# Softmax denominators of an eight-head attention: last four probability tiles summed by one strided reduction, in four pieces

## The reference, cut to what matters

```
s = einsum(qn, k_nope) + einsum(qr, k_rope)      # 1024 keys x 1024 queries for each head
p = softmax(s * scale, axis=-1)                  # exp(s - max) / sum over the keys of exp(s - max)
o = einsum(p, v)                                 # (1024 queries, 64) for each head
```

## Time and profile before

| | |
|---|---|
| median of 3 runs | 1615.19 us (1614.73 to 1616.01) |
| profiled execution, its own time | 1616.77 us |
| its span, first to last instruction | 1614.9 us |
| PE busy | 1500.5 us, 93% |
| DVE busy | 1072.1 us, 66% |
| ACT busy | 713.2 us, 44% |
| POOL busy | 426.7 us, 26% |
| mean granted TensorE clock | 0.968 |

### The profile page before, as it was taken

The page is one execution under the profiler, slowest core; times in us unless marked ns, Lnnn a source line. Parts: engine busy times, 40 slices in busy tenths (PEclk is TensorE's granted clock), DMA queues, the critical chain, the costliest instruction groups (busy, mean ns, idle before and its releaser), DMA issues.

```text
span 1614.9 us, 15669 instructions
## 1 busy us (share of the span) xinstructions
PE 1500.5 (93%) x5798; PEld 996.8 (62%) x5798; DVE 1072.1 (66%) x1022; ACT 713.2 (44%) x688; POOL 426.7 (26%) x209
## 2 busy tenths in 40 slices
PE   6999999999999999887899991799999999999997
PEld 3444587844344444444448871588888888887774
DVE  4533235433724656788766558598999998998886
ACT  3310000035503214433342442477777777777773
POOL 0031000000011006476764424022332222332204
PEclk9999999999999999999899995799999999999999
DMA  9311120206000000000013229699999999999994
GB/s 322 116 53 52 59 97 1 56 15 135 23 0 1 0 0 26 1 26 1 26 65 119 91 93 372 228 349 378 378 379 374 373 378 378 378 379 379 367 381 198
DMA packets 152886, 284.45 MB, mean 176 GB/s; under 512 B 25301, under 2 KB 35875, under 8 KB 152836
## 3 DMA queue, kind: packets, MB, share of 16 engines
q1 hardware_dynamic: 147219, 263.32, 45.9%
q0 software_dynamic: 4464, 16.25, 3.8%
q10 hardware_dynamic: 1152, 4.19, 0.6%
HBM read 259.10 MB, written 24.64 MB: 176 GB/s over the span
## 4 chain that ended last, share of the span: by engine, by line
PE 76%; DVE 11%; DMA 5%; issue 3%; ACT 2%; POOL 1%; SPq 0%; POOLq 0%; DVEq 0%; ACTq 0%
PE psum L1146 14%; PE psum L1602 9%; PE psum L1604 9%; PE psum L1603 9%; DMA arena<-in_exp_w_down 4%; PE psum L1377 4%; PE psum L1239 3%; PE psum L1127 3%; PE psum L1347 2%; PE psum L1092 2%; PE psum L1513 2%; PE psum L1439 2%; DVE arena L1917 2%; PE psum L1515 2%; PE psum L1514 2%
## 5 line engine op out<-in xcount | busy, mean ns | idle before, releaser
L2110 DVE TENSOR_TENSOR split_at<-arena,split_at 128x2048 fp32r<-128x2048 f32 x188 | 427.6, 2290 | 62.5 <-ACT split_at L1008 61.4
L1008 ACT ACTIVATE split_at<-arena 128x2048 fp32r<-128x2048 f32 x192 | 367.7, 1916 | 69.5 <-PE psum L1604 52.5
L1602 PE MATMUL psum<-split_at,split_at 128*128 128x512 f32 x768 | 305.9, 398 | 1.4 <-DVE split_at L2116 1.4
L1604 PE MATMUL psum<-split_at,split_at 128*128 128x512 f32 x768 | 300.2, 391 | 0.0
L1603 PE MATMUL psum<-split_at,split_at 128*128 128x512 f32 x768 | 299.5, 390 | 0.0
L1146 PE MATMUL psum<-arena 128*128 128x512 f32 x512 | 224.7, 594 | 1.4 <-DVE arena L1859 1.4
L1146 PEld LDWEIGHTS psum<-arena 128*128 128x128 f32 x512 | 96.1, 190 | 124.0 <-issue 123.9
L1604 PEld LDWEIGHTS psum<-split_at,split_at 128*128 128x128 f32 x768 | 144.5, 188 | 31.3
L1602 PEld LDWEIGHTS psum<-split_at,split_at 128*128 128x128 f32 x768 | 144.7, 188 | 29.7 <-DVE split_at L2116 1.8
L1603 PEld LDWEIGHTS psum<-split_at,split_at 128*128 128x128 f32 x768 | 144.9, 189 | 28.4
L639 POOL COPY arena<-arena 128x1 uint32 (+1 forms) x14 | 28.3, 2021 | 361.2 <-DVE arena L2144 361.2
(11 more groups left out here) (303 smaller groups left out, 2299.3 us busy)
## 6 DMA issues: line engine op xcount, KB each, us to landing
arena<-in_exp_w_gate SPq DMA_DIRECT2D x64, 1024.0 KB, 14.8
arena<-in_exp_w_up SPq DMA_DIRECT2D x64, 1024.0 KB, 14.2
arena<-in_exp_w_down SPq DMA_DIRECT2D x64, 1024.0 KB, 14.3
arena<-in_w_in SPq DMA_DIRECT2D x9, 1024.0 KB, 8.5
arena<-in_x SPq DMA_DIRECT2D x8, 512.0 KB, 6.6
xhat_scratch<-arena SPq DMA_DIRECT2D x8, 512.0 KB, 9.9
arena<-in_w_out SPq DMA_DIRECT2D x8, 512.0 KB, 3.6
arena<-xhat_scratch SPq DMA_DIRECT2D x8, 512.0 KB, 4.7
```

The source lines that it names most:

```text
L1008: a(flat(wsplit[c % WS][0]), wraw[:, c], ACT.Copy).then_inc(s_whi, 1)
L1602: mm(bank(out_bank), src[0][:, k, :], whi[:, k % 4, :], start=(k == 0), stop=False)
L1604: ins = mm(bank(out_bank), src[1][:, k, :], whi[:, k % 4, :], start=False, stop=(k == KT - 1))
L2110: tt(flat(lo), wraw[:, c], flat(hi), ALU.subtract).then_inc(s_wlo, 1)
```

## The change

Five things are changed together.

1. DVE's three additions of tiles 4 to 7 are replaced by four `tensor_reduce` instructions. Each reads all four `p_at` tiles for 256 queries with the tile index innermost (consecutive elements lie 4096 bytes apart in a partition), adds the four, and writes 256 columns of `p_last`. All four wait for the head's last exponential and stand behind `max_rows(h + 1)`.
2. ACT's exponentials of units 0 to 3 of a head now wait for all four pieces of the head before (`s_da` at `4 h`).
3. `sums_inverse` writes its result back into bank 7; `o_scale` reads it there and not from SBUF. The PE waits that protect bank 7 are on `s_ov` (the scaling) and no longer on `s_oi` (the inverse). `o_scale(h - 1, 0)` stands ahead of `max_rows`, `o_scale(h - 1, 1)` behind the pieces.
4. `p_first` has two buffers, by head parity. POOL's first addition waits for the sums of head `h - 2`.
5. `sum_probs(h, 0)` moves from the end of head `h` into head `h + 1`, directly ahead of `sum_probs(h, 1)`. SP's loads into `gin`, `bin_` and `xres` wait for head 6's sums.

```
-        p_first, p_last = mem(27600, T), mem(29648, T)
-        o_raw, o_inv = mem(30672, 2, HALF), mem(52176, 2, HALF)
+        p_first, p_last = [mem(28624, T), mem(27600, T)], mem(29648, T)
+        o_raw = mem(30672, 2, HALF)
...
-            sp.wait_ge(s_exp, TT * (NH - 1))
+            sp.wait_ge(s_sum, 2 * NH - 2)
...
-                if i == 0 and h:
-                    pool.wait_ge(s_sum, 2 * h - 1)
+                if i == 0 and h >= 2:
+                    pool.wait_ge(s_sum, 2 * h - 2)
...
-                        act.wait_ge(s_da, 3 * h - 3 + max(kb, 1))
+                        act.wait_ge(s_da, 4 * h)
...
                 if part == 0:
                     pe.wait_ge(s_pa, 3 * h + 3)
                     if h:
-                        pe.wait_ge(s_oi, 2 * h)
+                        pe.wait_ge(s_ov, 2 * h)
                 else:
-                    pe.wait_ge(s_da, 3 * h + 3)
+                    pe.wait_ge(s_da, 4 * h + 4)
...
                         if m == 0 and h:
+                            sum_probs(h - 1, 0)
                             sum_probs(h - 1, 1)
...
-                sum_probs(h, 0)
                 if more:
                     scores(TT * h + TT)
                     scores(TT * h + TT + 1)
+            sum_probs(NH - 1, 0)
             sum_probs(NH - 1, 1)
...
                 if i == 0:
-                    pe.wait_ge(s_oi, 2 * NH)
+                    pe.wait_ge(s_ov, N_OUT + 4)
...
-                v.reciprocal(o_inv[:, h % 2, cols], bank(7)[:, cols]).then_inc(s_oi, 1)
+                v.reciprocal(bank(7)[:, cols], bank(7)[:, cols]).then_inc(s_oi, 1)
...
-                   o_inv[half, h % 2, c0:c1], ALU.mult).then_inc(s_ov, 1)
+                   bank(7, 1, DV * j, DV * j + DV)[:, c0:c1], ALU.mult).then_inc(s_ov, 1)
...
+            def add_probs(h, c):
+
+                v.wait_ge(s_exp, TT * h + TT)
+                if h:
+                    v.wait_ge(s_sum, 2 * h)
+                cols = slice(256 * c, 256 * c + 256)
+                v.tensor_reduce(p_last[:, cols], p_at[:, :, cols].rearrange("p b t -> p t b"), AX.X, ALU.add).then_inc(s_da, 1)
...
-                add_probs(h, 0)
-                if h + 1 < NH:
+                if h:
+                    o_scale(h - 1, 0, 0, HALF)
+                if more:
                     max_rows(h + 1)
-                add_probs(h, 1)
-                add_probs(h, 2)
+                for c in range(4):
+                    add_probs(h, c)
                 if h:
-                    for j in range(2):
-                        o_scale(h - 1, j, 0, HALF)
+                    o_scale(h - 1, 1, 0, HALF)
```

More of the change, by code:

```diff
@@ L577, in add_probs @@
                 pool.wait_ge(s_exp, TT * h + i + 2)
-                if i == 0 and h:
-                    pool.wait_ge(s_sum, 2 * h - 1)
+                if i == 0 and h >= 2:
+                    pool.wait_ge(s_sum, 2 * h - 2)
                 if i:
                     pool.wait_ge(s_pa, 3 * h + i)
-                first = p_at[:, 0, :] if i == 0 else p_first
-                pool.tensor_tensor(p_first, first, p_at[:, i + 1, :], ALU.add).then_inc(s_pa, 1)
+                total = p_first[h % 2]
+                pool.tensor_tensor(total, p_at[:, 0, :] if i == 0 else total, p_at[:, i + 1, :], ALU.add).then_inc(s_pa, 1)
             for h in range(NH):
@@ L1447, in sum_probs @@
                     if h:
-                        pe.wait_ge(s_oi, 2 * h)
+                        pe.wait_ge(s_ov, 2 * h)
                 else:
-                    pe.wait_ge(s_da, 3 * h + 3)
+                    pe.wait_ge(s_da, 4 * h + 4)
                 for j in range(2):
-                    ins = mm(bank(7, 1, DV * j, DV * j + DV), ones[:, 0:DV], (p_first, p_last)[part][:, HALF * j:HALF * j + HALF],
+                    ins = mm(bank(7, 1, DV * j, DV * j + DV), ones[:, 0:DV], (p_first[h % 2], p_last)[part][:, HALF * j:HALF * j + HALF],
                              start=(part == 0), stop=(part == 1))
@@ L1966, in o_scale @@
                 tt(yT_at[DV * (h % 2):DV * (h % 2) + DV, h // 2, HALF * j + c0:HALF * j + c1], o_raw[half, h % 2, c0:c1],
-                   o_inv[half, h % 2, c0:c1], ALU.mult).then_inc(s_ov, 1)
[L1969 to L1975, removed]
+                   bank(7, 1, DV * j, DV * j + DV)[:, c0:c1], ALU.mult).then_inc(s_ov, 1)
[5 more added lines that the diff above has]
+                v.tensor_reduce(p_last[:, cols], p_at[:, :, cols].rearrange("p b t -> p t b"), AX.X, ALU.add).then_inc(s_da, 1)
             for h in range(NH):
-                slots = (ROUGH_AT if h else ROUGH_AT_0) if h + 1 < NH else {}
+                more = h + 1 < NH
+                slots = (ROUGH_AT if h else ROUGH_AT_0) if more else {}
                 if h == 0:
```

## The result

The changed kernel takes **1634.2 us** (median of 4 runs, 1632.62 to 1635.97) against 1615.41 for the kernel before in the same session. The ratio is 1.0117, with a 95% interval from 1.0099 to 1.0134: 18.8 us slower. The forecast was 1604.6, faster. The measured time lies in the rival that the prediction called *something between* (1623 to 1637, chance 0.12).

The account below looks back on a forecast made before the run. DVE alone was taken to set the stretch at head boundaries, where PE stands waiting. From the median 1615.2 us: -26.0 + 3.3 + 4.4 + 7.7 = -10.6, so 1604.6; own range 1597 to 1611, full range 1597 to 1654.

Parts of the forecast that it names:

- something between: Rival: pieces at 1.5 times the price, or the first two slowed by POOL; 1623 to 1637 us, chance 0.12.
- the price of a piece: Each strided reduction on DVE: taken as 1.22 us, with bounds 1.22 and 2.29.
- a rival: Four pieces: a strided element costs twice the time, 2.29 us a piece; 1654 us, slower, chance 0.27.
- head 7 and the end: Last head up to `mix`: forecast +4.4 us, including +2.8 at head 7; +7 to +10 in something between.
- the stop at the end: After the last exponential: sums from 851.1 to 853.1, where `mix` starts; no clock loss counted.
- The scalings at 0.68: DVE at a head boundary: 0.7 us instead of 2.8 each with the inverse in PSUM; the first is free.
- no contention of the pieces with POOL: Pieces beside POOL's work: they stay at their own price, as a `tensor_reduce` never takes the shared port.
- the new wait of ACT: Next head's first exponential waits for all four pieces, starting at T+7.1 against about T+4.9; PE stands 2.8 us.
- the pieces and the scaling behind the last exponential: End of attention: pieces run from 845.4 to 850.4, head 6's second scaling to 851.1, then the sums.
- 1.1 us for each stop: Clock loss behind PE's new stop of 2.8 us in seven stretches: 0 to 1.5 each, 1.1 taken, +7.7 us.
- 5.1 us at each of boundaries 2 to 6: Five boundaries, heads 1 to 2 through 5 to 6: row maximum 2 at T+16.7 against T+21.8, -26.0 us in all.
- T+13.4: Row maximum of block 2 at the first boundary before; T is when DVE has a head's last row maximum; forecast +3.3.

Follow-up runs that it names:

- e1: Changed kernel with each of the four pieces reading 1024 side-by-side elements of one probability tile (denominators wrong): 1600.91 us, ratio to before 0.9914.
- e4: Changed kernel with 20 unused matmuls more on PE in each head but the first, ahead of score unit 2: 1620.82 us, ratio to before 1.0039.
- e2: Kernel before, with the inverse kept in bank 7, scalings reading it there, both ahead of max_rows and the three additions behind it: 1579.0 us, ratio 0.9774.
- e3: Changed kernel with the three chained additions in place of the four strided pieces, and ACT's old waits: 1602.29 us, ratio to before 0.9914.
- e7: Changed kernel with three chained additions for the pieces, ACT's old waits, and both scalings ahead of max_rows: 1582.38 us, ratio to before 0.9799.
- e10: As e3, with one useless DVE multiplication of 0.68 us ahead of the first scaling at each head's end: 1588.0 us, ratio 0.9831.
- e5: Changed kernel with each head's four pieces reading at steps of 8, 16, 32 and 128 bytes in place of 4096 (denominators wrong): 1630.6 us, timed once.
- e6: Changed kernel with each head's four pieces reading at steps of 64, 1024, 4080 and 4096 bytes: 1634.8 us, timed once.

## Why the prediction was wrong

**The step that failed** is the price of a piece: "I take 1.22", on the ground that fp32 elements at 1.04 ns each leave room for jumps. They do not: 1.92 us measured, 1.87 with the overlap. The prediction itself gave the break-even as 1.55 us a piece, named the mechanism in a rival and set that rival's price at 2.29. The truth lay at two thirds of the way, on the losing side, and fell into the case with a chance of 0.12. That case's sum holds where it was worked: -1.3 to +0.7 a boundary (0.0 measured) and +7 to +9 at the first (7.4). Only head 7 and the end were more, 14.0 against 7 to 10. That range was short by its own terms: 4.4, the slower pieces twice (2.1 to 2.9 each) and the clock (2 to 3) make 10.6 to 13.2. And the prediction gave the stop at the end no clock loss, while the sums there took 3.65 us in place of 1.9.

**What held.** The scalings at 0.68, free ahead of `max_rows`; no contention of the pieces with POOL (its two subtractions at the start of a head took 2.36 and 2.39 us beside them, medians of seven each, where the medians were 3.31 and 3.39 beside the additions; in e1 the pieces took 1.21 us beside the same work of POOL); the new wait of ACT, at which PE's stop was foreseen; the pieces and the scaling behind the last exponential. With the price of a piece at what I had taken, e1 measured 1600.9 against the 1604.6 of the forecast; the four then took 4.60 us and not 5.0, which at eight places is 3.2 of the 3.7 us. The stops were 2.2 us and not 2.8, and the clock fell behind five of the seven.

**The clock.** 1.1 us for each stop was near for a stop of 2.2 (0 or 1.4 in e1). For the stop of 5.08 it was 2.6 a boundary: filling the stop moved the mark by 2.4, with pieces that took 0.25 longer (e4). The forecast wanted 5.1 us at each of boundaries 2 to 6, before the clock. The dearer pieces took 2.5 of them (7.48 against 5.0) and the clock 2.6, and nothing was left, although DVE was done 3 us sooner. The size of the clock term hung on the price of the piece, which made the stop 5.08 us long and not 2.8.

**What I did not ask.** The prediction weighed the change as one thing. Its own rows held the 36 us that e2 gained: 5.6 us of scalings on the chain against 1.4, and a first boundary without them at T+13.4. It read the additions of 2.7 us rightly as slower beside POOL, but as a fixed price, while it is a price of who comes first (e3, e7, e10). It did not ask whether the scalings of 2.8 us are the same case; the pair of 1.41 us at heads 6 to 7 says that they are.

## What to carry to other kernels

An fp32 reduction on DVE whose consecutive elements lie 16 bytes or more apart took 1.5 to 1.6 times a sequential one here: count that before a strided reduction takes the place of sequential additions. One instruction that needs all of several buffers also gives them back all at once, and whoever refills the first of them waits for the whole. Where DVE and POOL meet on SBUF, see which of them asks first: moving 0.7 us of work by one place was worth 20 us (e3 to e7), and moving the scalings with one operand kept in PSUM 36 us (e2), against the 18.8 that the change lost.

## What the runs showed of the hardware that was not expected

- The price of a strided fp32 reduction of 1024 elements is a step, not a slope: 1.22 us at 8 bytes, 1.86 to 1.98 us from 16 bytes to 4096 (e5, e6).
- Such reads get slower still beside PE's work: the four took 7.73 us with 20 more matmuls beside them against 7.48 (e4), and the last of them 1.97 to 2.0 us against 1.87. Sequential pieces did not move (1.206 to 1.221 us over all 32 of e1).
- The lower clock can come or not behind the same stop of 2.2 us: four of six boundaries of one execution of e1 had it and two had not, by the granted clock (0.65 to 0.67 against 1.00 over the 5 us behind the stop) and by their marks.
- DVE and POOL, both with operations whose two inputs lie in SBUF, alternate instruction by instruction once both wait: 8.19 against 6.02 us for three additions (e3, e7), and 7.90 against 6.02 within one execution (e10), decided by 0.1 us of arrival.
- A DVE multiplication of 64x512 with both inputs in SBUF took 0.70 us with POOL idle and 2.8 beside POOL's additions, in the same execution of the kernel before.
